# DSA and MLA softmax on Trainium2: mask, factor and the row's minimum of the negated logits in one VectorE operation

## The reference, cut to what matters

```
# DSA: one block of 128 queries
logits = einsum('bthd,btkhd->bthk', qb, k_sel) * (dh ** -0.5) + bias
logits = where(valid, logits, -inf)
probs  = softmax(logits, axis=-1)

# MLA
s = einsum('bhqd,bhkd->bhqk', q_b, k) * (DN + DR) ** -0.5   # 192 ** -0.5
# causal mask, softmax, times v
```

## Time and profile before

| | |
|---|---|
| Median of 3 executions | 901.88 us (901.68 to 904.54) |
| The profiled execution, its own time | 900.74 us |
| Its span, first to last instruction | 898.9 us |
| TensorE matmuls busy | 861.6 us (96%), x5768 |
| VectorE busy | 683.7 us (76%), x1090 |
| ScalarE busy | 449.3 us (50%), x712 |
| Mean granted TensorE clock | 0.992 |

### The profile page before, as it was taken

The page is one execution under the profiler, slowest core; times in us unless marked ns, Lnnn a source line. Parts: engine busy times, 40 slices in busy tenths (PEclk is TensorE's granted clock), DMA queues, the critical chain, the costliest instruction groups (busy, mean ns, idle before and its releaser), DMA issues.

```text
span 898.9 us, 14495 instructions
## 1 busy us (share of the span) xinstructions
PE 861.6 (96%) x5768; PEld 755.3 (84%) x5768; DVE 683.7 (76%) x1090; ACT 449.3 (50%) x712; POOL 69.0 (8%) x62
## 2 busy tenths in 40 slices
PE   8999989999999999989999999899999899999996
PEld 8988977677876887789899999679987799999995
DVE  5598799878977997789866856796887876656657
ACT  5464554454556545366545445264553665455450
POOL 1000001000001120001200100110000021001001
PEclk9999999989999999999999999999999999999999
DMA  9855567545965870699866797278716885655601
GB/s 337 298 169 195 193 232 240 184 142 197 340 236 211 279 258 1 245 359 354 314 214 230 266 361 262 80 270 318 242 58 247 304 323 184 203 175 185 191 1 47
DMA packets 57028, 201.00 MB, mean 224 GB/s; under 512 B 6600, under 2 KB 7936, under 8 KB 56960
## 3 DMA queue, kind: packets, MB, share of 16 engines
q1 hardware_dynamic: 55952, 196.89, 62.5%
q0 software_dynamic: 1008, 3.18, 1.1%
HBM read 198.96 MB, written 1.08 MB: 223 GB/s over the span
## 4 chain that ended last, share of the span: by engine, by line
PE 81%; DVE 12%; ACT 3%; issue 3%; POOL 0%; DMA 0%; DVEq 0%; ACTq 0%
PE ps L1160 26%; PE ps L1161 25%; PE ps L1162 25%; DVE R L1471 2%; DVE wsp L1408 2%; PE ps L1173 1%; DVE small L1675 1%; PE ps L1345 1%; PE ps L1376 1%; DVE wk L1446 1%; PE ps L1252 1%; PE ps L1352 1%; PE ps L1337 0%; PE ps L1243 0%; DVE pb L1666 0%
## 5 line engine op out<-in xcount | busy, mean ns | idle before, releaser
L1160 PE MATMUL ps<-XT,wsp 128*128 128x256 f32 x768 | 217.3, 283 | 3.9 <-DVE XT L1453 3.0
L1161 PE MATMUL ps<-XT,wsp 128*128 128x256 f32 x768 | 214.5, 279 | 0.0
L1162 PE MATMUL ps<-XT,wsp 128*128 128x256 f32 x768 | 214.2, 279 | 0.0
L1408 DVE TENSOR_TENSOR wsp<-ring,wsp 128x1024 fp32r<-128x1024 f32 x144 | 178.1, 1244 | 9.3 <-ACT wsp L1954 9.3
L1954 ACT CAST wsp<-ring 128x1024 fp32r<-128x1024 f32 x143 | 148.6, 1044 | 61.7 <-PE ps L1162 54.9
L1160 PEld LDWEIGHTS ps<-XT,wsp 128*128 128x128 f32 x768 | 144.0, 187 | 8.4 <-issue 3.9
L1161 PEld LDWEIGHTS ps<-XT,wsp 128*128 128x128 f32 x768 | 144.0, 187 | 0.9
L1162 PEld LDWEIGHTS ps<-XT,wsp 128*128 128x128 f32 x768 | 143.7, 187 | 0.0
L1160 PE MATMUL ps<-wsp,ra 128*128 128x512 f32 x236 | 94.6, 401 | 4.0 <-issue 1.5
L1162 PE MATMUL ps<-wsp,ra 128*128 128x512 f32 x236 | 93.6, 397 | 0.0
L1161 PE MATMUL ps<-wsp,ra 128*128 128x512 f32 x236 | 93.1, 394 | 0.0
(11 more groups left out here) (269 smaller groups left out, 1530.7 us busy)
## 6 DMA issues: line engine op xcount, KB each, us to landing
arena<-in_mod_w SPq DMA_DIRECT2D x50, 512.0 KB, 6.0
ring<-in_mod_w SPq DMA_DIRECT2D x42, 512.0 KB, 4.9
ring<-in_ffn_a SPq DMA_DIRECT2D x28, 512.0 KB, 4.9
ring<-in_ffn_b SPq DMA_DIRECT2D x28, 512.0 KB, 5.2
arena<-in_ffn_o SPq DMA_DIRECT2D x22, 512.0 KB, 4.6
ring<-in_ffn_o SPq DMA_DIRECT2D x22, 512.0 KB, 4.8
arena<-in_ffn_a SPq DMA_DIRECT2D x16, 512.0 KB, 5.9
arena<-in_ffn_b SPq DMA_DIRECT2D x16, 512.0 KB, 4.6
```

Of the source, the lines that this page charges most:

```text
L1160: pe.matmul(o, l[0], r[0], start=start, stop=False)
L1161: pe.matmul(o, l[0], r[1], start=False, stop=False)
L1162: return pe.matmul(o, l[1], r[0], start=False, stop=stop)
L1408: ve.tensor_tensor(w[:, 1024:1024 + n], raw[slot[0]][:, 0:n], w[:, 0:n].bitcast(f32), SUB).then_inc(*done("V", "lo", u, also=[("raw", *slo ...
```

## The change

In DSA and MLA the two VectorE instructions of a softmax item, the one that masks and the `tensor_reduce`, become one `tensor_tensor_reduce`. It writes p = (scores + mask) * c, with c = -1 in DSA and c = -(192^-0.5) in MLA, and gives the minimum of p over the row, seeded with 3e38, to the column of `nmx`. Since p holds the negated logits, their minimum is the negated maximum. ScalarE's exp gets the factor -1.0 in these two tasks: exp(-p + nmx). MOBA keeps its two instructions; its exp gets the factor 1.0. The event `logit` is gone for DSA and MLA: the bank is given back with the event `nmx`. No step is moved in the list, and no DMA, matmul or tile is changed.

```diff
-                        ve.tensor_tensor(p, ps[b[0]][:, 0:n], scr[:, (2 * t + 1) * 256:(2 * t + 1) * 256 + n], ADD
-                                         ).then_inc(*done("V", "logit", task, i, also=freed))
+                        ve.tensor_tensor_reduce(p, ps[b[0]][:, 0:n], scr[:, (2 * t + 1) * 256:(2 * t + 1) * 256 + n],
+                                                -1.0, 3e38, ADD, MIN, nmx[:, i:i + 1]).then_inc(
+                            *done("V", "nmx", task, i, also=freed))
                     elif task == "mla":
                         for e in new("V", ("fill", *b), before):
                             ve.wait_ge(*e)
-                        ve.scalar_tensor_tensor(p, ps[b[0]][:, 0:n], 192.0 ** -0.5, C("cm", 256 - n, 256), MUL,
-                                                ADD).then_inc(*done("V", "logit", task, i, also=freed))
+                        ve.tensor_tensor_reduce(p, ps[b[0]][:, 0:n], C("cm", 256 - n, 256), -(192.0 ** -0.5), 3e38, ADD,
+                                                MIN, nmx[:, i:i + 1]).then_inc(*done("V", "nmx", task, i, also=freed))
                     else:
                         for e in new("V", ("fill", *b), before, ("dist", 1)):
                             ve.wait_ge(*e)
                         ve.scalar_tensor_tensor(p, dist[:, t, 0:n], -(2.0 ** -(h + 1)), ps[b[0]][:, 0:n], MUL,
                                                 ADD).then_inc(*done("V", "logit", task, i, also=freed))
-                    for e in new("V", ("logit", task, i)):
-                        ve.wait_ge(*e)
-                    ve.tensor_reduce(nmx[:, i:i + 1], p, AX.X, MAX, negate=True).then_inc(*done("V", "nmx", task, i))
+                        for e in new("V", ("logit", task, i)):
+                            ve.wait_ge(*e)
+                        ve.tensor_reduce(nmx[:, i:i + 1], p, AX.X, MAX, negate=True).then_inc(*done("V", "nmx", task, i))
...
-                    ac.activation(p, p, ACT.Exp, bias=nmx[:, i:i + 1], accum_out=smx[:, i:i + 1]).then_inc(
-                        *done("A", "exp", task, i))
+                    ac.activation(p, p, ACT.Exp, bias=nmx[:, i:i + 1], scale=1.0 if task == "moba" else -1.0,
+                                  accum_out=smx[:, i:i + 1]).then_inc(*done("A", "exp", task, i))
```

More of the change, by code:

```diff
@@ L951 @@
     tensor_tensor = tensor_scalar = scalar_tensor_tensor = tensor_copy = tensor_reduce = tensor_tensor_scan = op
-    max = match_replace = bn_stats = bn_aggr = op
+    max = tensor_tensor_reduce = match_replace = bn_stats = bn_aggr = op
 def build(nc, D, out):
```

## The result

The changed kernel takes 894.98 us (median of 4 executions, 893.48 to 896.32) against 902.86 us for the kernel before beside it (4 executions, 901.68 to 904.54). The ratio is 0.9917, 95% interval 0.9899 to 0.9935. The forecast was 893.0 us, the range 891.3 to 899.0. The profiled execution took 893.48 us, 7.26 us less than the one before.

The account below looks back on a forecast made before the run. TensorE was taken as the bound (81% of the span), VectorE deciding only in short stretches. DSA 1.85 + 2.4 = 4.25 and MLA 4.9 made 9.1 us; 901.88 - 9.1 = 892.8, taken as 893.0, range 891.3 to 899.0.

Parts of the forecast that it names:

- rivals 3 and 4: Fused operation at the scan's rate, saving 0.09 us an item (899.9, chance 0.08); or slower than the pair (904 to 908.5, 0.06).
- the read: On VectorE, writing the row's minimum after each fused operation was taken to cost 0.10 us, bounds nothing and 0.19.
- rival 2: Writing the minimum costs 0.19 us or above; VectorE saves 3.1 us an attention: 895.4, or 897.7 with both clock falls; chance 0.13.
- ScalarE's factor: In exp, the factor -1.0 costs nothing; if it cost 0.05 us, ScalarE's 2.47 us of idling before it would cover that.
- The first steps: In DSA, fused items before `gated` close all but 0.1 of a 1.57 us stall; TensorE's transposes start 1.85 us earlier.
- the clock that stayed up: In DSA from 180.75 on, TensorE gains 0.9 us on the transposes and 1.5 on `w_moz`, together 2.4.
- After 186 TensorE sets the pace and VectorE has waits again, so what is won stays: In DSA after 186, nothing of the 4.25 us won is given back.
- the freeing of banks: Banks freed by `nmx` some 0.1 us later cost nothing, as scores are issued ahead; otherwise 32 x 0.1 us at stake.
- the clock's part: In MLA behind the stall ending at 334.77, TensorE gains 1.7 us if the clock stays up.
- The forecast's ceiling for TensorE: In MLA, TensorE's idle times and lost clock, 2.0 + 1.7 + 0.46 + 1.2 = 5.4 us, let it follow VectorE's 4.9.
- Rival 1: The clock falls all the same in DSA (895.2 us), MLA (894.1) or both (896.5); chance 0.27 in all.
- the likeliest case: Main case, clock kept up in both DSA and MLA: 893.0 us, own range 891.5 to 894.3, chance 0.42.

Follow-up runs that it names:

- MOBA fused: Changed kernel with the same fusion carried to MOBA, each head's factor put into its queries: 893.44 us, ratio 0.9891 to the kernel before.
- `hm0` later: Changed kernel with the DSA transposes that fill PSUM banks 0 and 1 moved two row blocks later: 894.32 us, ratio 0.9903 to the kernel before.
- both edits: Changed kernel with the DSA transposes moved later and MOBA fused as well: 890.99 us, ratio 0.986 to the kernel before.
- MLA alone: Changed kernel with DSA given its two instructions back, fused only in MLA: 897.91 us, ratio 0.9938 to the kernel before.
- DSA alone: Changed kernel with MLA given its two instructions back, fused only in DSA: 900.36 us, ratio 0.9971 to the kernel before.
- without the minimum: Changed kernel with one plain masking instruction and no row maximum in DSA and MLA, exp without bias: 893.91 us, ratio 0.9902 to the kernel before.
- spare reduction: Changed kernel with an unread VectorE reduction of a constant tile behind each fused operation in DSA and MLA: 898.59 us, ratio 0.995 to the kernel before.

## Why the prediction was right, and where it was not

**The price of the fused operation.** The rate was right: 413 to 419 ns, elementwise, so rivals 3 and 4 fall. The Trainium skill ("DVE: opcode table, instruction layouts, handler registers and perf-mode slots", section "Datapath and trigger behaviour") has a stage that reads its own last result run without a bubble, and these rows agree. The halved rate that the Trainium skill ("Vector Engine (DVE) Microarchitecture Reference", section "Points that are easy to get wrong") states for two wide sources in SBUF does not show here, where one source is in PSUM. The page states it of another instruction than this custom one, and no run here tried both sources in SBUF. The term that was mis-sized is the read: 0.10 us taken, 0.00 measured, its lower bound. VectorE saves 6.0 us an attention in place of 4.6, and rival 2 falls (its second time, 897.7, is 897.4 by its own terms). ScalarE's factor cost nothing, as forecast: exp over 256 columns lasts 0.51 us before and after. The reason given for it doesn't hold, though: idle time before exp is no cover for a longer exp, since VectorE's reciprocal waits for exp's end, as the rows under MLA show.

**DSA: 2.98 us in place of 4.25.** The first steps came out, and the first one larger. The seven transposes started 180.75 - 135.89 = 44.86 us behind mark 1 before, and 179.74 - 137.15 = 42.59 after: 2.27 us won, where 1.85 was forecast and six items with a free read give 4 x 0.45 + 2 x 0.30 = 2.4. From there to TensorE's next head it took 5.86 us before (180.75 to 186.61) and 3.63 after (179.74 to 183.37): 2.23 us for the clock that stayed up, against the forecast 2.4. The first row is before, the second after:

```profile
186.61 0.38 PE L1352 MATMUL ps<-cst,pb 128*128 128x128 f32 x2
183.37 0.38 PE L1352 MATMUL ps<-cst,pb 128*128 128x128 f32 x2
```

The step that failed is "After 186 TensorE sets the pace and VectorE has waits again, so what is won stays". At that head TensorE was 4.5 us early (186.61 - 183.37 = 3.24, and 1.26 more since mark 1 is that much later); then it came to the scores that use banks 0 and 1 behind `hm0` before these were empty and gave 1.44 us back. Moving `hm0` shows that a wait there is not one of order alone: in its place come 0.69 us for ScalarE's copy and 0.53 for VectorE's multiply, and only 0.7 us is won. In the forecast the freeing of banks was looked at for the scores' own reader, not for the transposes' readers that share the banks.

**MLA: 5.90 us in place of 4.9.** The path was the forecast one: VectorE sets the pace to the last item. Its last multiply starts 357.78 - 257.94 = 99.84 us behind mark 3 before and 350.14 - 256.20 = 93.94 after, 5.90 us earlier, and the transpose of TensorE that awaits it (358.12 and 350.48) as much:

```profile
357.78 0.29 DVE L1684 TENSOR_SCALAR pb<-pb,small 128x128 f32<-128x128 f32 x1
...
350.14 0.28 DVE L1685 TENSOR_SCALAR pb<-pb,small 128x128 f32<-128x128 f32 x1
```

The term that was too small is again the read: with it free the items save 6.0 us in place of 4.6. On VectorE's timeline three smaller things come to it. A wait of 0.37 us for the scores (before 339.28) is gone, forecast as 0.3. Waits for ScalarE's L2123 shrank by 0.1 us in three heads. And 0.7 us are lost again: in five of the eight items of 128 columns the reciprocal comes 0.35 us behind the start of the fused operation in place of 0.22, since it waits for ScalarE. ScalarE's read of the row's sum, from 331.69, ends at 331.88:

```profile
331.55 0.28 DVE L1667 CUSTOM_DVE_ANT_0 pb<-ps,cst 128x128 f32<-128x128 f32 x1
331.76 0.08 DVE L1667 DVE_READ_ACCUMULATOR2_ANT small<- 128x1 f32 x1
331.91 0.16 DVE L1682 RECIPROCAL small<-small 128x1 f32<-128x1 f32 x1
```

On TensorE's side the 5.90 us come in three parts. Up to the end of the long stall (334.77 and 331.69) it is 1.34; the stall was forecast at about 0.85 us and is 0.79. From there to the same step of the next head, 339.23 before and 334.49 after, it takes 4.46 and 2.80 us, 1.66 less: that is the clock's part, forecast as 1.7. Before, the clock was at 0.50 through most of it; after, it is at 1.00. The same four matmuls take 1.91 us and 1.03:

```profile
337.33 1.91 PE L1345 MATMUL ps<-arena 128*128 128x256 f32 x4
339.23 0.39 PE L1376 MATMUL ps<-pt,arena 128*128 128x128 f32 x2
...
333.52 1.03 PE L1345 MATMUL ps<-arena 128*128 128x256 f32 x4
334.49 0.39 PE L1376 MATMUL ps<-pt,arena 128*128 128x128 f32 x2
```

The last 2.90 us are waits that went behind it: the 0.46 and the 1.20, and some 1.3 us that the profile counts as busy, as it does where a matmul stands waiting for a moment (L1160 at 351.40 lasts 0.50 us, its counterpart at 345.15 0.40). The forecast's ceiling for TensorE, 5.4 us, left these out and was too low.

**The clock.** Rival 1 didn't come about in the profiled execution, but it is no settled matter. With the same DSA list the clock near 188 stayed at 1.00 in the changed kernel and fell with MOBA fused, whose first edited instruction runs at 259 us; likewise with `hm0` later it fell and with both edits it didn't. The lengths differ by 65.67 - 64.05 = 1.62 us and 64.95 - 63.33 = 1.62 us. That is the price of a fall there. The changed kernel's four executions point to falls as a part of their spread of 2.8 us: 893.48 us goes with a mean granted clock of 0.996 and 896.32 with 0.993. Where in them the clock fell isn't recorded. Nor does the argument against rival 1 hold, that TensorE idled 1.20 us without a fall: behind an equal wait in MOBA the clock fell in two profiles (672.20 in MLA alone, 1.20 us; 671.06 with `hm0` later, 1.19 us) and stayed up in the changed kernel (668.20).

**A place that was not in the forecast.** Near 122 us TensorE stalls for 2.26 to 2.28 us in all kernels of this study, before any changed instruction. In the profile of before the clock stays up behind it, in that of the changed kernel it doesn't:

```profile
122.00:124.00 2.00, 1.83 (x7) 1.45 (x8) 1.63 (x4) 1.24 (x2) 0.00 (x0) 0.84 0.12 47
124.00:126.00 2.00, 2.00 (x6) 1.52 (x5) 1.97 (x5) 0.00 (x0) 0.00 (x0) 0.50 0.23 37
126.00:128.00 2.00, 2.00 (x9) 1.60 (x8) 1.83 (x9) 0.23 (x1) 0.00 (x0) 0.80 0.97 365
```

From the end of that stall to mark 1 it is 13.76 us before (122.13 to 135.89), 13.78 with DSA alone and without the minimum, and 14.98 in the changed kernel (122.17 to 137.15): a fall costs 1.2 us. It came in seven of the nine profiles taken after the change, with equal code up to there, and the one profile of before has none. Whether the change makes it likelier can't be told from that.

**The sum.** 2.98 + 5.90 = 8.9 us where the code was changed, against 9.1 forecast: DSA 1.3 too high and MLA 1.0 too low. That the sum came so near is luck, two misses that cancel. Less 1.26 before mark 1 and 0.36 behind mark 4 it is the 7.3 us of the profile. The medians say 7.9 us in the first comparison and 7.75 in the second, where 8.9 were forecast. The forecast of 893.0 was 2 us low: 1.0 is this, and 1.0 that the kernel before, measured again beside the changed one, had a median of 902.86 in place of 901.88. The result is inside the range, and a little outside the likeliest case's own range of 891.5 to 894.3. "The clock falls in a place that it did not before" was named as a sign of failure; it was seen, in a place that the change does not reach.

## What to carry to other kernels

Count an instruction's saving from the start of it to the start of the next, by the chain that waits for it: the removed wait between two dependent operations (0.11 us of the 0.45) counts beside the work, and for VectorE it was a quarter of what was saved. When a stall goes, follow the engine that is now early to the next buffer that it writes, with all the readers that must empty that buffer, those of other steps too; here 1.4 of 4.5 us went there. Busy time of TensorE holds short waits too, so what the clock cost is read from equal matmuls at both levels (1.66 us) and not from the fall of busy time (3.01). And read a stretch by marks at fixed places of one engine's list, since a fall of the clock elsewhere (1.2 or 1.6 us here) is as large as the effects that one is looking for.

## What the runs showed of the hardware

The instruction that writes a VectorE accumulator lasts 0.08 us and takes no step of VectorE, while ScalarE's lasts 0.19 us and delays the next by 0.09. Two VectorE operations over 256 columns take 0.79 us from start to start where the second waits for the first, and, with the spare reduction, 0.68 where it doesn't. A stall of TensorE does not settle by its length whether the clock falls from 2.4 to 1.2 GHz: behind 2.27 us near 122 the granted clock fell to 0.50 in seven profiles and stayed at 1.00 in three; behind 1.68 us near 335 it stayed up with the spare reduction; behind 1.20 us near 672 it fell in MLA alone.
